# A new order of gates and mixers in a two-layer hybrid encoder, and layer norm by token tile

## The reference

```
p = x @ w_in[l] + b_in[l]
branches = (attention_mixer(...), rwkv7_mixer(...), s5_mixer(...), mlstm_mixer(...))
for n in range(N_BRANCH):
    merged = merged + sigmoid(x @ w_gate[l, n] + b_gate[l, n]) * (branches[n] @ w_branch[l, n])
x = layer_norm(ALPHA * x + merged @ w_out[l], ln1_g[l], ln1_b[l])
ff = swiglu(...) if l % 2 == 0 else moe_swiglu(...)      # dense, or the best 2 of 8 experts
x = layer_norm(ALPHA * x + ff, ln2_g[l], ln2_b[l])
```

## Time and profile before

| what | value |
|---|---|
| time, median of 3 runs | 2055.73 us (2051.96 to 2061.02) |
| profiled execution | 2052.61 us, its span 2050.2 us |
| TensorE, VectorE, ScalarE busy | 1903.7, 692.8, 325.6 us |
| mean granted TensorE clock | 0.965 of 2.4 GHz |
| read from HBM | 468.68 MB |

### The profile page before, as it was taken

The page is one execution under the profiler, slowest core; times in us unless marked ns, Lnnn a source line. Parts: engine busy times, 40 slices in busy tenths (PEclk is TensorE's granted clock), DMA queues, the critical chain, the costliest instruction groups (busy, mean ns, idle before and its releaser), DMA issues. The chain is left out here.

```text
span 2050.2 us, 65356 instructions
## 1 busy us (share of the span) xinstructions
PE 1903.7 (93%) x30112; PEld 1689.7 (82%) x30112; DVE 692.8 (34%) x1435; ACT 325.6 (16%) x745; POOL 101.3 (5%) x44
## 2 busy tenths in 40 slices
PE   8999788889999899978788899999999999999996
PEld 7777687657777677768664899999999999999995
DVE  7964472510211396356342211111111111111113
ACT  3232222010100323232120100000000000000001
POOL 4400000000100160000000000000000000000000
PEclk9999999899999999989979999999999999999998
DMA  7233211234444323321016599999999999999992
GB/s 288 101 103 123 83 43 43 74 121 154 154 153 143 123 103 124 119 87 43 2 66 252 207 396 400 398 398 400 393 415 392 403 400 395 402 404 401 400 400 82
DMA packets 54475, 470.98 MB, mean 230 GB/s; under 512 B 5184, under 2 KB 5456, under 8 KB 20336
## 3 DMA queue, kind: packets, MB, share of 16 engines
q1 hardware_dynamic: 37744, 292.04, 37.2%
q10 hardware_dynamic: 16272, 175.06, 21.0%
q0 software_dynamic: 368, 2.64, 0.3%
HBM read 468.68 MB, written 1.05 MB: 229 GB/s over the span
## 5 line engine op out<-in xcount | busy, mean ns | idle before, releaser
L1010 PE MATMUL bank<-arena,ring 128*64 128x88 f32 x8192 | 333.1, 239 | 0.0
L1010 PEld LDWEIGHTS bank<-arena,ring 128*64 128x64 f32 x8192 | 320.0, 137 | 0.0
L1010 PE MATMUL bank<-arena 128*64 128x88 f32 x6144 | 244.8, 239 | 0.6 <-DVE arena L1902 0.6
L1010 PEld LDWEIGHTS bank<-arena 128*64 128x64 f32 x6144 | 236.9, 137 | 1.2 <-issue 0.9
L771 PE MATMUL bank<-xT,ring 128*128 128x256 f32 x1024 | 229.4, 384 | 0.0
L1869 DVE TENSOR_TENSOR arena<-arena,bank 128x88 f32<-128x88 f32 x224 | 54.6, 244 | 514.3 <-ACT arena L1262 514.3
L771 PEld LDWEIGHTS bank<-xT,ring 128*128 128x128 f32 x1024 | 195.8, 192 | 32.4 <-issue 5.5
L1262 ACT ACTIVATE arena<-bank 128x88 f32<-128x88 f32 (+1 forms) x246 | 63.0, 256 | 921.6 <-PE bank L1010 726.6
L929 PE MATMUL bank<-arena,ring 128*64 128x88 f32 x4096 | 178.1, 239 | 0.2 <-issue 0.2
L929 PEld LDWEIGHTS bank<-arena,ring 128*64 128x64 f32 x4096 | 167.2, 137 | 4.7 <-issue 0.4
L450 PE MATMUL bank<-xT,ring 128*128 128x256 f32 x736 | 164.6, 386 | 3.2 <-DMA ring<-in_w_in 3.2
(11 more groups left out here) (418 smaller groups left out, 1791.4 us busy)
## 6 DMA issues: line engine op xcount, KB each, us to landing
ring<-in_moe SPq DMA_DIRECT2D x66, 1536.0 KB, 9.3
ring<-in_moe ACTq DMA_DIRECT2D x62, 1536.0 KB, 10.0
arena<-in_moe SPq DMA_DIRECT2D x49, 1536.0 KB, 9.6
arena<-in_moe ACTq DMA_DIRECT2D x47, 1536.0 KB, 9.4
ring<-in_ffn SPq DMA_DIRECT2D x22, 1536.0 KB, 6.5
ring<-in_w_gate SPq DMA_DIRECT2D x32, 1024.0 KB, 4.9
ring<-in_w_in SPq DMA_DIRECT2D x14, 1536.0 KB, 6.5
ring<-in_w_branch SPq DMA_DIRECT2D x8, 1024.0 KB, 4.8
```

The source lines that it names most:

```text
L1010: last = mm(bank[c:c + STRIP, g * CAP:(g + 1) * CAP], w[:, at:at + STRIP], rhs[:, kt, :], start=(kt == 0), stop=(kt == KT - 1), skip_group ...
```

## The change

- **Order of attention.** The head means and rotations, with their work on the other engines, move between the gates of branch 2 in `s5_end`. `attention` begins with the scores. Over the softmax stays gate (2,3) alone, where gates (0,0) to (0,3) were. Branch 2 is widened in one piece after the attention outputs, and its products on VectorE stand in the RWKV front. ScalarE scales the nine RWKV tiles ahead of the exps of the softmax; VectorE reads the attention outputs (`attention_out`) behind the token shift.
- **Order in RWKV.** The front's small products stand together (a, decay, value transposes, sum of squares, gate), followed by (0,0), bonus, (0,1), (0,2). Levels 1 to 5 of the inversion each have a gate in front: (0,3), (1,0), (1,1), (1,2), (1,3). One quarter of branch 0 follows each of the four scan steps, with its products on VectorE.
- **Order in mLSTM.** RWKV's mean, variance and output (`rwkv_mean`, `rwkv_variance`, `rwkv_centre`, `rwkv_out`) move into it. Gates (3,0), (3,1), (3,2), (3,3) stand behind the second scores, heads 0 and 1, and head 3. The tanh of the output gate (`ml_o`) moves beside the inversion.
- **Layer norm by token tile.** Statistics, root and application are done for tile 0, then tile 1. The root is a Sqrt on ScalarE and a reciprocal on VectorE; a Sqrt of one number stands ahead of them. The last unit of the output projection runs bank by bank; the last step of the dense mixer signals `dn_half` after two of its four products; the transposes behind it wait by tile.
- **Places in memory.** The mLSTM tiles, two gate chunks and a second product buffer `mg_t0` move, and GpSimd zeroes two more padded tiles.

The core of the diff (left out: moved lines that stay the same, and renamed bodies):

```diff
-MERGE_UNITS = [(2, 0), (2, 1), (2, 2), (2, 3), (2, 4), (0, 0), (0, 1), (0, 2), (0, 3), (0, 4), (1, 0), (1, 1), (3, 0),
-               (3, 1), (1, 2), (1, 3), (3, 2), (3, 3), (1, 4), (3, 4)]
+MERGE_UNITS = [(2, 0), (2, 1), (2, 2), (2, 3), (2, 4), (0, 0), (0, 1), (0, 2), (0, 3), (1, 0), (1, 1), (1, 2), (1, 3),
+               (0, 4), (3, 0), (1, 4), (3, 1), (3, 2), (3, 3), (3, 4)]
...
+        mg_t, mg_t0 = area(18816, 512), area(3840, 512)
...
-            return gate_old[:, k + 2, :] if br else gate_rw[:, k - 2, :]
+            if br:
+                return gate_old[:, k + 2, :]
+            return gate_old[:, 6, :] if k == 2 else brT[:, 2, :, :].rearrange("p a b -> p (a b)")
...
-        FILL_GATES = {1: (1, 2), 3: (1, 3)}
+        FILL_GATES = {1: (0, 3), 2: (1, 0), 3: (1, 1), 4: (1, 2), 5: (1, 3)}
...
-                branch(L, 2, range(2, 4))
-                for k in range(4):
-                    gate(L, 0, k)
+                gate(L, 2, 3)
...
             def rwkv(L):
-                branch(L, 0, range(4))
+                branch(L, 2, range(4))
...
-                gate(L, 1, 0)
...
-                gate(L, 1, 1)
...
-                gate(L, 3, 0)
-                gate(L, 3, 1)
+                pe.wait_ge(S["rw_sq"], L + 1)
+                b = open_bank(("rwss", L), "rw_ss")
+                fill(mm(b[:, :], C("sum64"), rw_gate2(), start=True, stop=True))
+                pe.wait_ge(S["rw_sg"], L + 1)
+                b = open_bank(("rwg", L), "rw_gate")
+                for q in range(2):
+                    last = mm(two(b)[:, q, :], M("g2", q * P, P), rw_sh[:, 7, :], start=True, stop=True)
+                fill(last)
+                gate(L, 0, 0)
+                pe.wait_ge(S["rw_bonus"], L + 1)
+                b = open_bank(("rwb", L), "dve_freed")
+                fill(mm(b[:, :], C("sum64"), rw_bonus_in(), start=True, stop=True))
+                gate(L, 0, 1)
+                gate(L, 0, 2)
...
+                    branch(L, 0, (s,))
+
+            def rwkv_mean(L):
...
+            def rwkv_variance(L):
...
-                gate(L, 3, 2)
...
             def s5_end(L):
 
                 gate(L, 2, 0)
+                head_means(L)
                 gate(L, 2, 1)
                 s5_read(L, 3)
+                rotations(L)
                 gate(L, 2, 2)
...
-                gate(L, 2, 3)
...
             def mlstm(L):
+                rwkv_mean(L)
...
                 scores(0)
-                gate(L, 3, 3)
+                rwkv_variance(L)
+                scores(1)
+                gate(L, 3, 0)
                 pe.wait_ge(S["ml_v"], L + 1)
                 for h in range(4):
-                    if h < 3:
-                        scores(h + 1)
                     branch(L, 1, (h,))
                     reads(h)
+                    if h < 2:
+                        scores(h + 2)
+                        gate(L, 3, h + 1)
+                gate(L, 3, 3)
                 pe.wait_ge(S["ml_h"], 4 * (L + 1))
...
+                    order = [(c, k) for c in range(2) for k in range(4)]
+                    if u == 3:
+                        order = [(c, k) for k in range(4) for c in range(2)]
+                    for c, k in order:
...
+                        if last_step and k == 1:
+                            last.then_inc(S["dn_half"], 1)
...
+                    transposed_x(2, lambda tt: pe.wait_ge(S["ln_z2"], 2 * tt + 2))
...
             def attention(L):
-                step(f(at_sq, proj[:, Q0:Q0 + 3, 2:2 + T], ACT.Square), "at_sq")
...
+                act.wait_ge(S["at_qr"], L + 1)
+                act.wait_ge(S["rw_params"], L + 1)
+                for j in range(9):
+                    ins = f(rw_sh[:, j, :], proj[:, R0 + j, 2:2 + T], ACT.Identity, scale=small[:, 32 + j:33 + j])
+                step(ins, "rw_scaled")
...
-                for k in range(4):
-                    gate(L, 0, k)
+                gate(L, 2, 3)
...
+                act.wait_ge(S["at_done"], 4 * (L + 1))
+                act.wait_ge(S["rw_kk"], L + 1)
+                step(f(flat(rw_cin)[:, 0:512], flat(rw_kk), ACT.Square), "rw_sq")
...
-                gate(L, 1, 0)
...
-                gate(L, 1, 1)
...
-                gate(L, 3, 0)
-                gate(L, 3, 1)
+                b = bank_of(act, ("rwss", L))
+                step(f(rw_AR.rearrange("p a b c d -> p (a b c d)")[:, 0:512], b[:, :], ACT.Sqrt), "rw_ss")
+                b = bank_of(act, ("rwg", L))
+                step(nc.scalar.copy(flat(rw_gate), b[:, :]), "rw_gate")
+                gate(L, 0, 0)
+                gate(L, 0, 1)
...
                 step(f(flat(rw_BT), flat(rw_cin), ACT.Exp, scale=-1.0), "rw_exp")
+                gate(L, 0, 2)
...
-                for k in range(3):
-                    gate(L, 2, k)
...
+                step(f(at_sq, proj[:, Q0:Q0 + 3, 2:2 + T], ACT.Square), "at_sq")
+                gate(L, 2, 0)
+                b = bank_of(act, ("ms", L, 0))
+                step(f(flat(at_rs[:, 0:2, :]), b[:, :], ACT.Ln, bias=EPS6), "act_freed")
+                b = bank_of(act, ("ms", L, 1))
...
+                step(f(flat(at_rs), flat(at_rs), ACT.Exp, scale=-0.5), "at_rs")
+                gate(L, 2, 1)
+                b = bank_of(act, ("v", L))
+                step(nc.scalar.copy(flat(at_v), b[:, 0:T]), "at_v")
+                act.wait_ge(S["s5_poly"], L + 1)
+                step(f(flat(s5_g), flat(s5_g), ACT.Tanh, scale=0.7978845608028654), "s5_th")
+                gate(L, 2, 2)
...
-                gate(L, 2, 3)
...
             def mlstm(L):
-                act.wait_ge(S["rw_done"], L + 1)
-                step(f(ml_so, proj[:, MO0:MO0 + 2, 2:2 + T], ACT.Tanh, scale=0.5), "ml_o")
+                act.wait_ge(S["rw_yc"], L + 1)
+                step(f(flat(rw_q), flat(rw_yc), ACT.Square), "rw_ysq")
...
-                for h in range(4):
+                b = bank_of(act, ("rwvar", L))
+                step(f(flat(rw_q), b[:, :], ACT.Ln, bias=EPSG), "act_freed")
+                step(f(flat(rw_q), flat(rw_q), ACT.Exp, scale=-0.5), "rw_rs")
...
+                scaled(0)
+                weights(0)
+                scaled(1)
+                weights(1)
+                gate(L, 3, 0)
+                for h in range(2):
+                    scaled(h + 2)
+                    gate(L, 3, h + 1)
+                    weights(h + 2)
+                gate(L, 3, 3)
...
             def norm(k, scale):
 
-                act.wait_ge(S["ln_sum"], TT * (k + 1))
-                step(f(ln_rstd, ln_mv[:, :, 1], ACT.Ln, scale=scale * scale, bias=EPSL))
-                step(f(ln_rstd, ln_rstd, ACT.Exp, scale=-0.5, bias=C("eps", 5 if scale == 0.5 else 6, 1)), "ln_rs")
+                f(small[:, 60:61], C("ones", 0, 1), ACT.Sqrt)
+                for tt in range(TT):
+                    act.wait_ge(S["ln_sum"], TT * k + tt + 1)
+                    step(f(ln_rstd[:, tt:tt + 1], ln_mv[:, tt, 1:2], ACT.Sqrt,
+                           bias=C("eps", 5, 1) if scale == 0.5 else EPSL), "ln_sd", hold=False)
...
-                products(L, 2, range(0, 2))
...
-                products(L, 2, range(2, 4))
...
+            def attention_out(L):
...
-                products(L, 0, range(4))
+                attention_out(L)
...
+                products(L, 2, range(0, 2))
...
+                products(L, 2, range(2, 4))
...
+                    products(L, 0, (s,))
+
+            def rwkv_centre(L):
                 b = bank_of(dve, ("rwmu", L))
...
+            def rwkv_out(L):
...
+                scale_heads(L)
...
+                rotate(L)
...
             def mlstm(L):
+                rwkv_centre(L)
...
+                exponents(0)
+                weights(0)
+                exponents(1)
+                rwkv_out(L)
                 for h in range(4):
-                    exponents(h)
+                    if h:
+                        weights(h)
+                        if h < 3:
+                            exponents(h + 1)
                     products(L, 1, (h,))
                     read(h)
                 b = bank_of(dve, ("mlo", L))
...
-                dve.wait_ge(S["ln_rs"], k + 1)
-                for tt in range(TT):
+                    dve.wait_ge(S["ln_sd"], TT * k + tt + 1)
+                    step(nc.vector.reciprocal(ln_rstd[:, tt:tt + 1], ln_rstd[:, tt:tt + 1]))
...
-                    dve.wait_ge(S["unit_used"], used_before["dense"] + FF_STEPS)
-                    norm(1, lambda tt, hf: banks[2 + 2 * tt + hf][:, :], 1.0, "ln_z2")
+                    dve.wait_ge(S["dn_half"], 1)
+                    norm(1, dense_sums, 1.0, "ln_z2")
```

More of the change, by code:

```diff
@@ L463, in project, with head_means @@
                         j += 1
-            def attention(L):
+            def head_means(L):
                 pe.wait_ge(S["at_sq"], L + 1)
@@ L471, in attention, with rotations @@
                 fill(mm(b[:, 0:T], C("mean64"), at_sq[:, 2, :], start=True, stop=True))
+            def rotations(L):
```

(28 more changed lines are left out.)

67 lines of the change are left out of this document (28 added, 39 removed).

## The result

The changed kernel takes 1971.9 us (median of 4 runs, 1968.56 to 1979.48), the kernel before 2054.68 beside it: a ratio of 0.9598, 95% interval 0.9561 to 0.9635. That is 82.8 us less, where 83.3 were the sum of the prediction. The profiled execution is the slowest of the four, 1979.48 us with a mean clock of 0.981; the others have 0.984 to 0.986. Differences read from its rows are therefore set against before's 2052.61, and they add up to only 73.1 us.

What follows compares the result with a forecast made beforehand. TensorE, busy 93% of the span, was taken as the bound, through its waits and clock. Terms 20.8 + 8.4 + 0 + 11.0 + 13.5 + 29.6 = 83.3 us off 2052.6 gave 1969 us; forecast 1948 to 1988 (0.68).

Steps and rivals of the forecast that it cites:

- Front, 20.8: From the projection's end to the scan's features: TensorE idle falls from 18.0 to 7.6 us a layer, 20.8 us in all.
- The features' 2.9: End of the RWKV front: of the 9.7 us wait for the scan's features, 2.9 us a layer stay.
- the value transpose's 3.1: RWKV front: new 3.1 us wait at the second value transpose, for banks held until VectorE's last two branch 2 products.
- the third quarter's 1.1: Branch 2's third quarter needs the first attention bank back from the ring of six: 1.1 us of new wait.
- Inversion and scan, 8.4: Five gates in the inversion instead of two cover VectorE's additions and masks, 8.4 us; branch 0 in the scan costed at nothing.
- mLSTM, 11.0: In the mLSTM stretch, new idle is 6.3 us a layer against 11.5 and 12.1 before: 11.0 us gained.
- Norms, 13.5: Four layer norms done by token tile, started before the preceding matmuls end, save 13.5 us together.
- Clock, 29.6: Filling TensorE's waits also lifts its clock, regaining nine tenths of the 32.9 us lost to the lower clock: 29.6 us.
- The idle goes but the clock stays: Rival: many short waits remain and keep TensorE's clock low, so only 53.7 us are gained: 1999 us, chance 0.13.
- Attention as the wait: Rival: softmax, with 20.8 us less cover, and late bank returns cost 10 us a layer: 1989 us, chance 0.12.
- No change and slower: Two rivals: weight stream takes the gain back, 2053 us, chance 0.03; low clock slows eight gates, 2081 us, chance 0.04.
- The walk is too cautious: Rival: branch 2's products arrive in time, features are covered, all the clock returns: 1952 us, part of the forecast's own range.

Runs made afterwards that it cites:

- p2: Changed kernel with VectorE's last two branch 2 products moved up behind rw_kk, and TensorE's bonus product ahead of gate (0,0): 1966.58 us.
- p4: As p3, and also ScalarE's exps of the features ahead of its reading of gate (0,1): 1953.19 us, ratio 0.9504.
- b1: Changed kernel with branch 0's four quarters and their products in one block behind the scan, not one quarter per step: 1974.76 us.
- p3: As p2, and also rwkv_out ahead of exponents(1), and branch 0's quarter between Z and U, its products ahead of the state sum: 1956.4 us.
- m1: Changed kernel with gates (3,1) and (3,2) taken from between the mLSTM heads and put ahead of (3,3), behind all reads: 1977.75 us.
- d1: Changed kernel without the small Sqrt in front of each norm that was to load the table ahead: 1973.39 us.
- w1: Kernel before, with matmuls that compute nothing placed in front of its long waits, order and all other work kept: 2031.1 us, ratio 0.9885.
- o1: The new order of gates and mixers with the old layer norm, against the kernel before: 1987.12 us, ratio 0.9672.
- s1: Changed kernel with gate (2,3) moved from the softmax to behind the attention outputs, on TensorE and ScalarE: 1983.67 us, ratio 0.9652.
- i1: Changed kernel with gates (0,3), (1,0), (1,1) in one block ahead of the features' wait, (1,2), (1,3) at inversion levels 1 and 3: 1973.97 us.

## Why the prediction was right

- **What bounds it.** Right: TensorE has the same records, and its idle and clock account for everything.
- **Front, 20.8.** Measured 23.1. The features' 2.9 were 2.80, the value transpose's 3.1 were 2.96, the third quarter's 1.1 was 0.71, and of the softmax's 0.5 nothing is seen. The features' wait was also right in its cause, ScalarE's order behind (0,1), which p2 and p4 show; the guess made after the result, that the bonus set it, fell with p2. The softmax had 2.3 us of slack that the walk did not see.
- **Inversion and scan, 8.4.** Measured 8.2, the 0.7 for the table switch and the 1.5 behind level 5 among what stays. Costing branch 0 in the scan at nothing was right (b1); that it could be placed to cover ScalarE's copies was overlooked (p3).
- **mLSTM, 11.0.** Measured 14.6. Branch 1's first quarter waits 2.01 and not 3.2, the variance nothing and not 0.6; head 3 (1.52 for 1.6) and the last 0.9 as given. One step was right in size and wrong in cause: "(3,1) and (3,2) each cover one head's exponents, exp, weights and reads". m1 shows that the waits of heads 1 and 2 stay away without these gates; the lead of two heads is the likely cause.
- **Norms, 13.5.** Measured 13.0. The two table loads were real: in the norm of the first output projection both stood behind the wait of the kernel before (430.41 and 432.02 us), in the other three only that of the Exp. The sentence on the dummy, "without it each would give back 1.3", was wrong for three of the four (d1).
- **Clock, 29.6.** This term was too large: it measured 18 to 24 us. By what is left of the medians it is 23.8, by w1 23.6, in place of nine tenths of 32.9; the first sets the idle time of the slowest execution against medians. Read directly, TensorE's busy time is 18.0 us less in the ten stretches, and 21.0 less over the span with the new order alone (o1). Only 73.1 - 59.0 = 14 us are left over in the profiled execution, because two stretches that the change leaves alone, the first projection and the dense mixer, were 1.9 and 1.5 us longer in it. The step "nearly all of these stretches hold gates now" failed in the scan and the transposes: 0.89 in one scan, 0.88 behind the second layer's 2.8 us wait. It was made up by 5.8 us more of idle. That the sum came out within 0.5 us is luck: by the medians two terms missed by about 6 us each, in opposite directions.
- **The rivals.** "The idle goes but the clock stays" (1999) is out. Attention as the wait (1989) is out: it needed 10 us a layer, and even without its gate there are 4.8 (s1). No change and slower are out. "The walk is too cautious" was true by 5.8 us of its 14.

The Trainium skill, TensorE: Matmul & The Clock Gate, section "HAM oscillation — how this bites in real kernels", tells of recurring waits, long enough for that, behind which each following piece starts at the lower clock. The traces agree in part: behind 9.7 us of idle the transposes always ran slower, behind 2.8 us in 11 cases of 18 over all runs, and the changed kernel's inversion kept 1.00 through waits of 0.2 to 2.0 us.

## What to carry to other kernels

When filler work is dealt out over waits, count the waits and the fillers before arguing about places: i1 shows that a gate buys one wait wherever it stands, and w1 that part of what it buys is only TensorE's clock, which filler without any use bought as well. When an earlier result changes nothing (p2), look at the order of the engine that reads it next: here it sat idle in front of a gate while the chain's input lay ready, and one swap on ScalarE halved the wait. And judge a gate by taking it away, not by the wait that went when it came: the same edit had also moved the scores.

## What the runs showed of the hardware

- **The clock varies between executions of one program.** The changed kernel's scan had 0.89 in the first layer and 1.00 in the second, with the same waits inside it; the kernel before had 1.00 and 0.86, w1 0.84 and 1.00, p2 and p4 1.00 twice. Four runs of the changed kernel spread over 11 us, in the order of their mean clocks (0.981 to 0.986). p4, which has no wait over 1.5 us in the mixers, spread over 4.3. The effect of small waits on the mean and on the spread may be one thing; no run was made for that alone.
- **A table load can run ahead of the wait of the function that needs it,** here by 6 to 36 us in three of four places. In the kernel before it is the same: the load for its Ln came behind the wait in the norm of the first output projection alone. What decides that place is open.
- **The transposes of 64 x 64** took 3.95 us for 128 records at 1.00, 6.45 behind 9.7 us of idle, and 5.44 behind 2.80 in the second layer. Over all profiles the four behind 9.7 us took 6.37 to 6.53; of the 18 behind 2.8 us seven took 3.95 and eleven 5.25 to 5.50, sometimes one of each in one execution; the six behind 1.4 us or less (p4, w1, i1) all took 3.95. The two layers of the changed kernel:

```profile
191.87 3.95 PE L560 MATMUL bank<-cst,arena 64*64 64x64 f32 x128 [2.80 <-DVE arena L1585]
...
832.65 5.44 PE L560 MATMUL bank<-cst,arena 64*64 64x64 f32 x128 [2.80 <-DVE arena L1585]
```
